# GpSimd's order in the second and fourth down projection: the last two adding transfers before the squares of X

## Chip, cores and metric

One core of a Trainium2 chip runs the whole forward pass of a small model in one launch. The metric is the device time of one launch in microseconds. The kernel before takes 1082.13 us, the median of three runs (1081.0 to 1082.24). The engines are named TensorE (PE), VectorE (DVE), ScalarE (ACT), GpSimd (POOL) and SyncE (SP), whose queue issues most loads.

## The reference

The input x has 512 tokens of 1024 features. There are two layers. The first mixes tokens by sliding-window attention, the second by gated linear attention, and each is followed by a gated feed-forward block (FFN) with 2816 hidden features:

```python
def conv_ffn(h, w_up, conv_w, conv_b, w_down):
    u = h @ w_up
    gate, up = u[..., :D_FF], u[..., D_FF:]
    ...
    return (jax.nn.silu(conv) * up) @ w_down

for i in range(DEPTH):
    h = rmsnorm(x, mix_norm[i])
    ...
    x = x + y
    x = x + conv_ffn(rmsnorm(x, ffn_norm[i]), f_w_up[i], f_conv_w[i], f_conv_b[i], f_w_down[i])
return rmsnorm(x, final_norm)
```

What matters here is `h @ w_down`, its addition to x, and the RMS norm behind it, which needs the sum of x squared over the 1024 features of each token. All is in float32.

## The kernel before

**Layout.** X lies with features on the 128 partitions, as 8 tiles of 128 x 512 (features x tokens). Every float32 matmul is made of three faster ones: operands are split into a high part (a cast, made by ScalarE) and a low part (raw minus high, made by VectorE), and high x high, high x low and low x high are summed in PSUM.

**The FFN** runs in two chunks of hidden features: 6 pairs of 128-feature tiles in the first chunk, 5 pairs in the second (`PAIRS`). For each chunk the up projection runs first and the down projection behind it. The down projection is computed with a Strassen-like scheme: the 256 x 256 block of a round is made of seven products (`PRODUCTS`: Z1, W11, W12, Z2, Z4, Z3, W22) of 128 x 256 matmuls. W11, W12 and W22 are quarters of the weight as loaded; Z1 = W21 + W22 and Z3 = W21 + W11 are sums made by transfers; Z2 = Z1 + W11 and Z4 = Z2 + W12 are sums made by VectorE (`sum_z2`, L1496; `sum_z4`, L1505).

**Rounds.** A chunk has four rounds, n to n + 3, one for each pair of X tiles. Rounds are numbered through the kernel: 0 to 3 and 4 to 7 are layer 0's two chunks, 8 to 11 and 12 to 15 layer 1's. "Second and fourth down projection" are rounds 4 to 7 and 12 to 15. TensorE's order is written out in `down_phase` (L590): within the second round of a chunk it is Z1, W22 of the round before, W11, W12, Z2, Z4, Z3, and then the next round's Z1. In a second chunk each product is 5 x 3 matmuls of 256 columns.

**The sums by transfer.** SP loads W21 into a buffer (`load_21`, L351). GpSimd waits for it (`first_half`) and issues a transfer that adds W22 or W11 to it in place (`add_quarter`, L1992). The buffers of the last round, n + 3, are loaded by SP in `load_round` (L374) when the first round's W22 is done, in the middle of the second round; those of the earlier rounds lie in GpSimd's queue before. ScalarE (`weight_hi`, L1013) and, for Z1, VectorE (`sum_z2`) wait for the added sum.

**The squares.** In a second chunk the rounds complete X tile by tile. ScalarE's `down_round` (L1073) calls `x_tile` (L972): the high part of the finished X tile in layer 0, and its square into one of two buffers SQ (L980). It writes a buffer only after GpSimd has summed the square of two tiles before. GpSimd's `sum_square` (L1974) copies square 0 to SS (L1981) and adds the others to SS (L1984). Squares 0 and 1 are of the first round's two tiles, 2 and 3 of the second's, 4 and 5 of the third's.

**VectorE's order** (`down_rounds`, L1602). Takes (`take_z4`, `take_z3` and others, L1522) add or subtract a product's PSUM bank to a half of an X tile. Between them VectorE makes the low parts of the weights (`weight_lo`, L1494), sum_z2 (L1503) and sum_z4 (L1514). In the second round m = n + 1 it goes, after take_z2: sum_z2 of m + 1, low part of Z1 of m + 1, take_z4, sum_z4 of m + 1, low part of W11 of m + 1, and then, as the next round's first step, take_z3 of m. TensorE needs the low part of Z1 before Z1 of the third round, and take_z3 before W22 of the second, which uses the same PSUM bank:

```python
def w22(n, between=None):
    pe.wait_ge(x_taken, COUNT[n, "Z3"])
    down_product(n, "W22", SETS[n % 2][0], False, between=between)
```

**GpSimd's order** is `ffn` in its block (L1987): squares 6 and 7 of the norm ahead of the FFN, then in each chunk the eight adding transfers, and in a second chunk squares among and behind them.

Of the kernel before, what the change touches and what calls it, by code (L numbers as in the profile page):

```python
# [95 lines left out]
def trunk(nc, xT, gains, w_qkv, sinks, rel_bias, w_o, w_bin, w_ga, w_gate, b_norm, w_bo, w_up, conv_w, conv_b,  # L96
          w_down0, w_down1, onehot, ident, causal, causal_pair, out, bias_rows):
    with ExitStack() as ctx:
# [202 lines left out]
        def down_cols(n):  # L301

            return PAIRS[n // 4 % 2] * P

        def quarter(n, name):

            layer, chunk, r = n // 8, n // 4 % 2, n % 4
            return (w_down0, w_down1)[chunk][layer, r, ("W11", "W12", "W21", "W22").index(name)]

        def with_sum(n, name):  # L310

            if n % 4 == 0:
                return DRAW["Z1"] if name == "Z1" else Z3RAW
            return WSUM[name, n % 4]
# [1650 lines left out]
        def _(pool):  # L1965
# [8 lines left out]
            def sum_square(st, m, par=None):  # L1974

                par = m % 2 if par is None else par
                pool.wait_ge(sq_ready, m + (KT_D * st + 1))
                if isinstance(m, int) and m == 0:
                    if st:
                        pool.wait_ge(std_ready, st)  # L1980
                    nc.gpsimd.tensor_copy(SS[:], SQ[:, 0]).then_inc(ss_ready, 1)  # L1981
                    pool.wait_ge(ss_ready, KT_D * st + 1)
                else:
                    nc.gpsimd.tensor_tensor(SS[:], SS[:], SQ[:, par], ALU.add).then_inc(ss_ready, 1)  # L1984
                    pool.wait_ge(ss_ready, m + (KT_D * st + 1))

            def ffn(layer, st):  # L1987
                for j in range(2):
                    sum_square(st, 6 + j)
                pool.wait_ge(r_ready, st + 1)  # L1990

                def add_quarter(n, name):  # L1992
                    onto, src = with_sum(n, name), "W22" if name == "Z1" else "W11"
                    pool.wait_ge(first_half[name, n % 4], 16 * (n // 4 + 1))
                    pool.dma_start(onto[:, 0:down_cols(n)], quarter(n, src), accum_op=ALU.add)\
                        .then_inc(added[name, n % 4], 16)

                for chunk in range(2):
                    n = 4 * (2 * layer + chunk)
                    for m in range(n, n + 3):  # L2000
                        add_quarter(m, "Z1")
                        add_quarter(m, "Z3")
                    if chunk:
                        sum_square(st + 1, 0)
                    add_quarter(n + 3, "Z1")
                    if chunk:
                        sum_square(st + 1, 1)
                    add_quarter(n + 3, "Z3")
                    if chunk:
                        for m in range(2, 6):  # L2010
                            sum_square(st + 1, m)
                if layer == 0:
                    for m in (6, 7):
                        sum_square(st + 1, m)
# [26 lines left out]
            for m in range(6):  # L2041
                sum_square(1, m)
            ffn(0, 1)
            pool.wait_ge(down_done, COUNT[7, "W22"])
            nc.gpsimd.memset(GAT[:].bitcast(F32), 1.0).then_inc(small_set, 2)
# [39 lines left out]
            for m in range(6):  # L2085
                sum_square(3, m)
            ffn(1, 3)

            pool.wait_ge(sq_ready, KT_D * 5 - 1)
# [88 lines left out]
```

## Time and profile before

| what | value |
|---|---|
| median of 3 runs | 1082.13 us (1081.0 to 1082.24) |
| the profiled execution's own time | 1082.68 us |
| its span, first to last instruction | 1080.9 us |
| TensorE busy | 1071.6 us, 99% |
| VectorE busy | 751.2 us, 69% |
| ScalarE busy | 494.3 us, 46% |
| GpSimd busy | 113.4 us, 10% |
| granted TensorE clock, mean | 1.000 |
| down projection, second chunk of layer 0 | from 453.31 us |
| down projection, second chunk of layer 1 | from 1020.55 us |

The durations come from one profiled execution, with times from its first instruction. Matmuls overlap each other, so that the distance between the starts of two says more than the duration of one. A row of a timeline has the start, the duration, the engine, the line of the kernel, the operation, what it writes and reads, the shapes, and in brackets the idle time before it with what ended it.

### The profile page before, as it was taken

How to read it: one execution, taken by the hardware profiler on the slowest of the kernel's cores; microseconds unless marked ns; L12 is line 12 of the kernel's file. 1: busy time of each engine (PE TensorE's matmuls, PEld its weight loads, DVE VectorE, ACT ScalarE, POOL GpSimd, SP SyncE). 2: the span in 40 equal slices, each digit the busy share in tenths (PEclk: the TensorE clock that was granted, in tenths of full speed). 3: DMA queues.
4: the chain of work that ended last, by engine and by line, in shares of the span. 5: the costliest groups of instructions: out<-in, count | busy, mean ns of one | idle time of the engine just before them, and what ended most of it. 6: DMA issues, size and time to landing. Idle time of an engine off the chain costs nothing.

```text
span 1080.9 us, 15711 instructions
## 1 busy us (share of the span) xinstructions
PE 1071.6 (99%) x5930; PEld 920.9 (85%) x5930; DVE 751.2 (69%) x1097; ACT 494.3 (46%) x769; POOL 113.4 (10%) x108
## 2 busy tenths in 40 slices
PE   9999999999999999999999999999999999999997
PEld 7888788888899888899888888888888899888897
DVE  6588667676876667789644556867676876667785
ACT  7366554444443334455661345454444433334443
POOL 1100030000100000123021221130000100000122
PEclk9999999999999999999999999999999999999999
DMA  7611032225652225652222211232226652225552
GB/s 228 153 59 60 27 111 98 97 97 184 161 145 98 96 97 170 141 154 91 79 78 98 79 40 59 66 110 98 97 97 184 161 149 97 94 97 170 139 135 91
DMA packets 43804, 121.12 MB, mean 112 GB/s; under 512 B 5250, under 2 KB 10530, under 8 KB 43748
## 3 DMA queue, kind: packets, MB, share of 16 engines
q1 hardware_dynamic: 36020, 106.55, 28.8%
q0 software_dynamic: 4608, 11.54, 6.4%
q10 hardware_dynamic: 3120, 2.28, 1.2%
q8 instruction: 37, 0.61, 0.2%
q14 instruction: 19, 0.16, 0.1%
HBM read 116.93 MB, written 2.88 MB: 111 GB/s over the span
## 4 chain that ended last, share of the span: by engine, by line
PE 96%; DVE 1%; ACT 1%; DMA 1%; issue 0%; SPq 0%; POOL 0%; DVEq 0%; POOLq 0%
PE PS L485 70%; PE PS L545 19%; PE PS L667 1%; PE PS L685 1%; PE PS L849 1%; PE PS L675 1%; DMA X<-xT 1%; PE PS L817 1%; PE PS L851 0%; PE PS L836 0%; PE PS L820 0%; PE PS L746 0%; PE PS L773 0%; PE PS L859 0%; PE PS L786 0%
## 5 line engine op out<-in xcount | busy, mean ns | idle before, releaser
L485 PE MATMUL PS<-XH,WH 128*128 128x512 f32 x992 | 391.3, 394 | 1.0 <-DVE WL L1700 0.6
L485 PE MATMUL PS<-XH,WL 128*128 128x512 f32 x992 | 386.4, 390 | 0.0
L485 PE MATMUL PS<-XL,WH 128*128 128x512 f32 x992 | 386.1, 389 | 0.0
L485 PEld LDWEIGHTS PS<-XH,WH 128*128 128x128 f32 x992 | 186.3, 188 | 41.8 <-issue 2.9
L485 PEld LDWEIGHTS PS<-XL,WH 128*128 128x128 f32 x992 | 186.3, 188 | 38.9 <-issue 1.0
L485 PEld LDWEIGHTS PS<-XH,WL 128*128 128x128 f32 x992 | 186.2, 188 | 39.0
L950 ACT CAST WH<-WRAW 128x1024 fp32r<-128x1024 f32 x134 | 139.5, 1045 | 158.1 <-DMA WRAW<-w_up 107.5
L1389 DVE TENSOR_TENSOR WL<-WRAW,WH 128x1024 fp32r<-128x1024 f32 x134 | 167.4, 1250 | 16.4 <-ACT WH L950 15.8
L1427 DVE TENSOR_TENSOR GS<-PS,R 128x512 f32<-128x512 f32 x44 | 30.4, 692 | 118.2 <-PE PS L485 118.2
L545 PE MATMUL PS<-AH,DH_Z 128*128 128x256 f32 x352 | 97.9, 278 | 0.3
L545 PE MATMUL PS<-AH,DL_Z 128*128 128x256 f32 x352 | 97.4, 277 | 0.0
L545 PE MATMUL PS<-AL,DH_Z 128*128 128x256 f32 x352 | 97.3, 277 | 0.0
L993 ACT ACTIVATE CV<-GS,CONVB,CONVW 128x512 f32<-128x512 f32 x44 | 36.0, 819 | 91.6 <-DVE GS L1427 91.6
L545 PE MATMUL PS<-AH,DH_W 128*128 128x256 f32 x264 | 73.7, 279 | 0.1
L545 PE MATMUL PS<-AL,DH_W 128*128 128x256 f32 x264 | 73.0, 277 | 0.0
L545 PE MATMUL PS<-AH,DL_W 128*128 128x256 f32 x264 | 73.0, 277 | 0.0
L1522 DVE TENSOR_TENSOR X<-X,PS 128x256 f32<-128x256 f32 x112 | 46.3, 418 | 35.2 <-PE PS L545 34.7
L545 PEld LDWEIGHTS PS<-AH,DH_Z 128*128 128x128 f32 x352 | 66.2, 188 | 2.2 <-PE PS L485 1.9
L545 PEld LDWEIGHTS PS<-AL,DH_Z 128*128 128x128 f32 x352 | 66.1, 188 | 0.0
L545 PEld LDWEIGHTS PS<-AH,DL_Z 128*128 128x128 f32 x352 | 66.1, 188 | 0.0
L1027 ACT CAST DH_W<-DRAW_W 128x768 fp32r<-128x768 f32 (+1 forms) x48 | 37.0, 780 | 53.3 <-DMA DRAW_W<-w_down 53.1
L545 PEld LDWEIGHTS PS<-AH,DH_W 128*128 128x128 f32 x264 | 49.7, 188 | 0.5 <-DVE X L1522 0.4
(236 smaller groups left out, 1513.0 us busy)
## 6 DMA issues: line engine op xcount, KB each, us to landing
WRAW<-w_up SPq DMA_DIRECT2D x88, 512.0 KB, 3.2
WRAW<-w_bin SPq DMA_DIRECT2D x24, 512.0 KB, 3.2
DRAW_W<-w_down SPq DMA_DIRECT2D x24, 384.0 KB, 3.8
DRAW_W<-w_down SPq DMA_DIRECT2D x24, 320.0 KB, 3.0
WSUM_Z<-w_down SPq DMA_DIRECT2D x12, 384.0 KB, 4.8
WSUM_Z<-w_down POOLq DMA_DIRECT2D x12, 384.0 KB, 6.1
WRAW<-w_qkv SPq DMA_DIRECT2D x8, 512.0 KB, 3.5
WSUM_Z<-w_down SPq DMA_DIRECT2D x12, 320.0 KB, 3.9
```

The costliest lines, as they stand in the source:

```text
L485: last = mm(PS[:, bank], w[:, c:c + P], x[:, kb], start=start and n == 0 and w is wh and x is hi, stop=stop and n == len(kbs) - 1 and w is wl)
L545: last = mm(PS[:, bank, 0:TH], w[:, c], act_part[:, kb, x], start=start and kb == 0 and w is DH[name] and act_part is AH, stop=kb == PAIRS ...
L667: last = mm(PS[:, B4 + k % 2, c:c + P], q, keys[:, first:first + P], start=True, stop=True)
L675: last = nc.tensor.transpose(PS[:, B6, i * P:(i + 1) * P], PB[:, k % 2, i], IDENT[:])
L685: last = mm(PS[64 * half:64 * half + 64, B7, j * P:(j + 1) * P], V[:, 1 - j if p else 0, p, g * HD:(g + 1) * HD], PT[:, k % 2, 2 * j + hal ...
L817: mm(PS[:, B4, c], EN[:, h, c], EP[:, h, c], start=True, stop=True)
L950: nc.scalar.copy(WH[s][:], WRAW[s][:]).then_inc(hi_ready, 1)
L993: A(CV[:, par], GS[:, par, 2:T + 2], ACT.Identity, bias=CONVB[:, layer, tile], scale=CONVW[:, layer, tile, 2]).then_inc(c0_ready, 1)
L1027: nc.scalar.copy(DH[name][:, c], raw[:, c]).then_inc(down_hi[name], 1)
L1389: tt(WL[s][:], WRAW[s][:], WH[s][:].bitcast(F32), ALU.subtract).then_inc(lo_ready, 1)
L1427: tt(GS[:, par, 2:T + 2], PS[:, 2 * par], R[:], ALU.mult).then_inc(unit_evac, 2)
L1522: tt(x, x, PS[:, SETS[n % 2][bank], 0:TH], op).then_inc(x_taken, 1)
```

## The change

In the second chunk of each layer GpSimd issued the adding transfers of the last round with squares 0 and 1 between them. It now issues both transfers directly behind the six before, and sums squares 0 to 5 behind them. Nothing else is changed.

```diff
@@ -2000,14 +2000,10 @@
                     for m in range(n, n + 3):
                         add_quarter(m, "Z1")
                         add_quarter(m, "Z3")
-                    if chunk:
-                        sum_square(st + 1, 0)
                     add_quarter(n + 3, "Z1")
-                    if chunk:
-                        sum_square(st + 1, 1)
                     add_quarter(n + 3, "Z3")
                     if chunk:
-                        for m in range(2, 6):
+                        for m in range(6):
                             sum_square(st + 1, m)
                 if layer == 0:
                     for m in (6, 7):
```

## Rows read from the trace of the kernel before

**Rows 1.** The page, part 1: busy time, share of the span and instructions.

```profile
PE 1071.6 (99%) x5930; PEld 920.9 (85%) x5930; DVE 751.2 (69%) x1097; ACT 494.3 (46%) x769; POOL 113.4 (10%) x108
```

**Rows 2.** Timeline of TensorE, layer 0: last matmul of Z1, first of W22.

```profile
477.22 0.28 PE L545 MATMUL PS<-AH,DL_Z 128*128 128x256 f32 x1
477.47 0.38 PE L545 MATMUL PS<-AH,DH_W 128*128 128x256 f32 x1
```

**Rows 3.** Timeline of TensorE, layer 1: around the starts of Z1 and W22.

```profile
1042.77 0.28 PE L545 MATMUL PS<-AH,DL_Z 128*128 128x256 f32 x1
1043.12 0.36 PE L545 MATMUL PS<-AH,DH_Z 128*128 128x256 f32 x1
...
1044.81 0.28 PE L545 MATMUL PS<-AH,DL_Z 128*128 128x256 f32 x1
1045.16 0.38 PE L545 MATMUL PS<-AH,DH_W 128*128 128x256 f32 x1
```

**Rows 4.** Timeline of VectorE, layer 0: sum_z2, low part of Z1, take_z3.

```profile
473.51 1.04 DVE L1503 TENSOR_TENSOR DRAW_Z<-WSUM_Z,DRAW_W 128x640 f32<-128x640 f32 x1 [0.65 <-DMA DRAW_W<-w_down]
474.47 0.81 DVE L1494 TENSOR_TENSOR DL_Z<-WSUM_Z,DH_Z 128x640 fp32r<-128x640 f32 x1
...
477.00 0.41 DVE L1522 TENSOR_TENSOR X<-X,PS 128x256 f32<-128x256 f32 x1
```

**Rows 5.** Timeline of VectorE, layer 1: the same three operations.

```profile
1040.41 1.83 DVE L1503 TENSOR_TENSOR DRAW_Z<-WSUM_Z,DRAW_W 128x640 f32<-128x640 f32 x1 [0.30 <-DMA DRAW_W<-w_down]
1042.16 0.81 DVE L1494 TENSOR_TENSOR DL_Z<-WSUM_Z,DH_Z 128x640 fp32r<-128x640 f32 x1
...
1044.70 0.41 DVE L1522 TENSOR_TENSOR X<-X,PS 128x256 f32<-128x256 f32 x1
```

**Rows 6.** Timeline of GpSimd, layer 0: square 0, transfer, square 1, transfer.

```profile
466.89 0.61 POOL L1981 COPY SS<-SQ 128x512 f32<-128x512 f32 x1 [16.42 <-ACT SQ L980]
471.67 0.86 POOL L1995 DMA_DIRECT2D WSUM_Z<-w_down  x1 [4.16 <-DMA WSUM_Z<-w_down]
472.24 1.61 POOL L1984 TENSOR_TENSOR SS<-SS,SQ 128x512 f32<-128x512 f32 x1
474.26 0.89 POOL L1995 DMA_DIRECT2D WSUM_Z<-w_down  x1 [0.41 <-POOL SS L1984]
```

**Rows 7.** Timeline of GpSimd, layer 1: transfer, square 1, transfer.

```profile
1039.34 0.88 POOL L1995 DMA_DIRECT2D WSUM_Z<-w_down  x1 [4.90 <-DMA WSUM_Z<-w_down]
1039.90 1.64 POOL L1984 TENSOR_TENSOR SS<-SS,SQ 128x512 f32<-128x512 f32 x1
1041.95 0.89 POOL L1995 DMA_DIRECT2D WSUM_Z<-w_down  x1 [0.41 <-POOL SS L1984]
```

**Rows 8.** Timeline of all engines, layer 0, third round: a square and a low part.

```profile
489.96 1.29 POOL L1984 TENSOR_TENSOR SS<-SS,SQ 128x512 f32<-128x512 f32 x1 [6.19 <-ACT SQ L980]
490.03 1.90 DVE L1494 TENSOR_TENSOR DL_Z<-DRAW_Z,DH_Z 128x640 fp32r<-128x640 f32 x1
```

**Rows 9.** SP's loads of W21 for the last round, by line: layer 0, layer 1.

```profile
L353 SPq DMA_DIRECT2D WSUM_Z<-w_down x2: 432/432/433, 467.7 to 468.2; - x2
...
DMA to landing us min/median/max: 3.3/3.9/4.4
...
L353 SPq DMA_DIRECT2D WSUM_Z<-w_down x2: 432/432/432, 1035.0 to 1035.4; - x2
...
DMA to landing us min/median/max: 3.7/3.9/4.1
```

**Rows 10.** Timeline of ScalarE: the square of tile 2, layer 0 and layer 1.

```profile
477.64 0.61 ACT L980 ACTIVATE SQ<-X 128x512 f32<-128x512 f32 x1
...
1044.70 0.63 ACT L980 ACTIVATE SQ<-X 128x512 f32<-128x512 f32 x1
```

**Rows 11.** Stretches of 20 us, L545: PE busy (starts), PEld busy (starts), clock, DMA.

```profile
479.00:499.00 20.00, 20.00 (x179) 20.00 (x178) 1.00 0.37 120
...
1046.00:1066.00 20.00, 20.00 (x173) 20.00 (x172) 1.00 0.23 67
```

## The prediction

> **What bounds the kernel.** The page comes first: TensorE works 1071.6 of the span's 1080.9 us [rows 1]. So a change can only show where TensorE waits, or where it is made to wait. The change touches the two stretches in which the second column chunk of a layer is projected down, which begin near 453 us (layer 0) and 1020 us (layer 1), and there I read TensorE's timeline. Its matmuls of 256 columns follow each other about every 0.11 us (179 in 20 us, [rows 11]). Layer 0 has one visible wait, 477.22 to 477.47, where W22 of the second round starts late [rows 2]. Layer 1 has two in the same round: Z1 of the third round starts 0.35 us behind its forerunner, and W22 of the second again 0.35 [rows 3]. That is 0.14 us lost in layer 0 and 2 x 0.24 in layer 1.
>
> VectorE's timeline says what TensorE waited for. In layer 0 it is a chain of six operations without a gap: sum_z2, the low part of Z1, take_z4, sum_z4, the low part of W11, take_z3. It starts at 473.51, when a load lands, and ends at 477.41, and W22 starts 0.06 later [rows 4]. In layer 1 the chain runs from 1040.41 to 1045.11, and W22 starts at 1045.16 [rows 5]. It is 0.8 us longer there because sum_z2 takes 1.83 us instead of 0.81.
>
> GpSimd's timeline says why. Its square 1 is on SBUF from 1039.90 to 1041.54 [rows 7], and sum_z2, which reads two SBUF tiles, ends 0.70 later at 1042.24 [rows 5]. The pattern repeats: in layer 0 square 1 ends at 473.85 [rows 6] and sum_z2 at 474.55 [rows 4]. Later a square alone takes 1.29, and the subtraction begun 0.07 behind it takes 1.90 and ends 0.68 behind the square's end [rows 8]. So a VectorE operation on two SBUF tiles waits until a GpSimd operation is done, and then needs 0.70 instead of its 0.81: they overlap by about 0.12. Issuing a transfer does not do this: 0.89 us of issue from 474.26 leaves the subtraction at 474.47 with its 0.81 [rows 4, 6].
>
> **What the change does, and its cost.** It adds and removes no instruction. In each layer, squares 0 and 1 move behind the two transfers of the last round, on GpSimd's queue alone. SP's queue keeps its order.
>
> The transfers. Z1's issue waits for a landing now and stays at 471.67 and 1039.34 [rows 6, 7]. Z3's first half was issued at 468.2 and landed 4.4 us later, at 472.6; in layer 1 1035.4 + 4.1 = 1039.5 [rows 9]. GpSimd took up Z1 0.67 us after its landing (467.7 + 3.3 = 471.0 against 471.67), so Z3 can be issued at about 473.3 instead of 474.26, and in layer 1 right behind Z1's issue, at 1040.2 instead of 1041.95. That gain of 1.0 and 1.7 us is worth nothing: these sums are read for the last round, which TensorE has not begun. Z3's 320 KB then moves while the SP loads of the next round are in flight. Bounds: nothing, or the 1.1 us by which two issues half a microsecond apart differed in landing [rows 9], on a load with slack; I take nothing.
>
> The later squares and ScalarE. Square 0 must be summed before ScalarE writes the same buffer again, at 477.64 and 1044.70 [rows 10]. By the working below it is done at 474.8 and 1041.8 to 1042.4, so this wait stays covered, by over 2 us.
>
> The later squares and VectorE, which is the cost. Square 0, a copy of 0.61 us, ran at 466.89, where VectorE had time before its next operand from TensorE, and square 1 ended just as the chain began [rows 6]. Both now fall inside the chain.
> Layer 0: sum_z2 at 473.51 is no longer held and ends at 474.32. GpSimd leaves its issue at 474.2 and starts the copy behind it: 474.32 - 0.13 + 0.61 = 474.80. The low part of Z1 ends 0.69 later, 475.49. Square 1 follows: 475.49 - 0.13 + 1.29 = 476.65. take_z4 reads PSUM and slips in. sum_z4 ends at 476.65 + 0.69 = 477.34, the low part of W11 0.73 later, 478.07, take_z3 0.33 later, 478.40. It was 477.41: TensorE loses **1.0 us**.
> Layer 1: sum_z2 goes from 1040.41 to 1041.22. The issue ends at 1041.1, so the copy and the low part of Z1 compete for the next turn. Copy first: low part 1042.4, square 1 1043.6, sum_z4 1044.3, low part of W11 1045.0, take_z3 1045.3. Low part first gives 1045.3 too. It was 1045.11: TensorE loses **0.2 us**. Its wait for Z1 goes, but the one for W22, 1.7 us on, takes all of that back.
> Bounds: no loss at all if the squares were to find gaps, and 2 x (0.61 + 1.29) = 3.8 us if both lay in the chain twice over and nothing overlapped. I take 1.2 us, the value that the rows of this very chain give.
>
> The spacing behind a wait. From 1046 to 1066 TensorE starts 173 matmuls, from 479 to 499 it starts 179 [rows 11]: 3.4% fewer, at a granted clock of 1.00 both times, so it is no matter of the clock. Over the last 23 us this is 0.8 us. It began behind the wait at 1045.16. The wait in layer 0 left none. No row tells which wait leaves it. Both waits at W22 stay in place but end elsewhere, so it can go in layer 1 (-0.8) or come in layer 0, where 23 us of down projection follow as well (+0.8). I take 0 in both layers, as each layer's own row has it.
>
> **Sum.** The profiled execution took 1082.68 us, its span 1080.9: 1082.68 + 1.0 + 0.2 = 1083.9. The median of the runs shown, 1082.13, lies 0.55 below it, and so I forecast 1083.3.
>
> The handover weighed. The rows say that the loser of a collision ends 0.68 to 0.70 us behind the winner [rows 4 to 8], so the two overlap a little. The Trainium skill (SBUF - State Buffer, "Who interferes with whom" and "A bandwidth-pool intuition that's wrong") has the loser blocked until the other's end, plus about 115 ns in its one measurement. By that figure each of the eight handovers would cost about 0.24 us more, an estimate from that page, and the sum would be near 1085.2; the rows measure this handover without that gap.
>
> **Rivals.** 0.2% is 2.2 us, about what a measurement of this kernel can tell from no change; so "faster" is below 1080.0 and "slower" above 1084.3.
> - The wide spacing goes in layer 1: 1.2 - 0.8 = 0.4 us, 1082.5. For it: two of the three waits left none. Against: the wait at the same W22 did. Chance 0.25.
> - Slower: the wide spacing comes in layer 0 as well, from W22's start at 478.5 to 501. Its price is 0.8 us, 2.0 in all, 1084.1, and it decides if the longer wait (1.1 instead of 0.14 us) restarts TensorE as the one at 1045.16 did. Against: layer 0's present wait did not. Chance 0.18, and some two fifths of it beyond the bound.
> - The handover has no overlap: the loser needs its whole 0.81 or 1.29 behind the winner, 0.12 more at each of eight places, 1.0 us in all: 1084.3. All the collisions above speak against it. Chance 0.04, and half of it slower.
> - Faster: the squares fall behind the chain. Then all that VectorE lost to square 1 comes back, 0.14 + 0.48 + 0.8 = 1.4 us: 1080.7. It needs GpSimd to be held until 477.4 and 1045.1, some 3 us longer than two issues of 0.9 take, or ScalarE's square to be late. Nothing shows that. Chance 0.08, a third of it below the bound.
> - It does nothing: VectorE's delay meets slack that I don't see, or the order of the transfers alone was changed: 1082.1. Chance 0.10; the gapless chain of [rows 4] speaks against it.
>
> **The numbers.** My forecast has 0.35. Faster: 0.08 x 1/3, 0.03. Slower: 0.18 x 0.4 + 0.02 + 0.02 from the forecast's own tail = 0.11. The same: 0.86. The range goes from 1081.3, which leaves out most of the gaining case, to 1084.5, which takes in both spacings and the slower handover.
>
> **What would show it.** In the changed profile: Z3's issue about 1 us and 1.7 us earlier; squares 0 and 1 side by side behind it, near 474.2 and 1041.1; in layer 0 the low part of Z1 and sum_z4 stretched by about 0.4 and 0.8, and W22 starting at 478.5; in layer 1 sum_z2 back at 0.81, no wait before Z1, and W22 at 1045.4 on the old scale (plus what layer 0 added). It would be wrong if VectorE's chain were not stretched in layer 0, if ScalarE waited for square 0, or if the last 20 us held 179 matmuls instead of 173.

## The result and the profile after

The changed kernel takes 1084.34 us (median of 7 runs, 1083.52 to 1086.81), the kernel before in the same comparison 1081.8 us (7 runs, 1081.0 to 1082.24). The ratio is 1.0026, with a 95% interval of 1.0016 to 1.0036: slower by about 2.5 us. The forecast was 1083.3 us and no measurable change. The profiled execution of the changed kernel took 1084.34 us, its span 1082.5 us.

The page of the changed kernel, part 1, has TensorE's busy time almost where it was [rows 1], and GpSimd, whose instructions are the same 108, at 115.7 us instead of 113.4:

```profile
PE 1072.0 (99%) x5930; PEld 921.2 (85%) x5930; DVE 753.0 (70%) x1097; ACT 494.1 (46%) x769; POOL 115.7 (11%) x108
```

The view of TensorE's waits has a new first row. Its columns are the total wait in us, how often, and the longest. Both waits are for the low part of Z1, and it had no row before:

```profile
PE PS L545 <- DVE DL_Z L1494: 2.1, 2, 1.3
```

TensorE's timeline shows where: at Z1 of the third round in each layer, and a little again at W22 of the second. These rows stand against [rows 2, 3].

```profile
475.64 0.28 PE L545 MATMUL PS<-AH,DL_Z 128*128 128x256 f32 x1
476.71 0.35 PE L545 MATMUL PS<-AH,DH_Z 128*128 128x256 f32 x1 [0.80 <-DVE DL_Z L1494]
...
478.44 0.28 PE L545 MATMUL PS<-AH,DL_Z 128*128 128x256 f32 x1
478.75 0.38 PE L545 MATMUL PS<-AH,DH_W 128*128 128x256 f32 x1
...
1044.03 0.28 PE L545 MATMUL PS<-AH,DL_Z 128*128 128x256 f32 x1
1045.57 0.36 PE L545 MATMUL PS<-AH,DH_Z 128*128 128x256 f32 x1 [1.26 <-DVE DL_Z L1494]
...
1047.30 0.28 PE L545 MATMUL PS<-AH,DL_Z 128*128 128x256 f32 x1
1047.61 0.38 PE L545 MATMUL PS<-AH,DH_W 128*128 128x256 f32 x1
```

To compare executions I count from the first matmul of the stretch (453.31 and 1020.55 before, 453.06 and 1021.83 after). W22 of the second round started 24.15 us into the stretch in layer 0 and now starts at 25.69; in layer 1 it went from 24.61 to 25.78. That is 1.54 + 1.17 = **2.7 us**. From the last matmul of layer 0's stretch (line 545) to the first of layer 1's it is 519.27 us before and after, and from the last one of layer 1's stretch to the end of the span 9.27 and 9.25. So all of the loss lies in the two stretches that the change touches.

GpSimd's timeline, both layers, against [rows 6, 7]. The row "x2" holds both issues:

```profile
471.26 0.86 POOL L1995 DMA_DIRECT2D WSUM_Z<-w_down  x1 [21.14 <-DMA WSUM_Z<-w_down]
472.55 0.87 POOL L1995 DMA_DIRECT2D WSUM_Z<-w_down  x1 [0.43 <-DMA WSUM_Z<-w_down]
473.09 0.95 POOL L1981 COPY SS<-SQ 128x512 f32<-128x512 f32 x1
474.13 1.76 POOL L1984 TENSOR_TENSOR SS<-SS,SQ 128x512 f32<-128x512 f32 x1
...
1040.51 1.78 POOL L1995 DMA_DIRECT2D WSUM_Z<-w_down  x2 [21.64 <-DMA WSUM_Z<-w_down]
1041.88 1.03 POOL L1981 COPY SS<-SQ 128x512 f32<-128x512 f32 x1
1043.00 1.75 POOL L1984 TENSOR_TENSOR SS<-SS,SQ 128x512 f32<-128x512 f32 x1
```

VectorE's timeline of the same chain, against [rows 4, 5]:

```profile
473.03 1.70 DVE L1503 TENSOR_TENSOR DRAW_Z<-WSUM_Z,DRAW_W 128x640 f32<-128x640 f32 x1 [0.19 <-DMA DRAW_W<-w_down]
474.66 1.91 DVE L1494 TENSOR_TENSOR DL_Z<-WSUM_Z,DH_Z 128x640 fp32r<-128x640 f32 x1
476.49 0.41 DVE L1522 TENSOR_TENSOR X<-X,PS 128x256 f32<-128x256 f32 x1
...
478.29 0.41 DVE L1522 TENSOR_TENSOR X<-X,PS 128x256 f32<-128x256 f32 x1
...
1041.87 1.73 DVE L1503 TENSOR_TENSOR DRAW_Z<-WSUM_Z,DRAW_W 128x640 f32<-128x640 f32 x1 [0.51 <-DMA DRAW_W<-w_down]
1043.53 1.90 DVE L1494 TENSOR_TENSOR DL_Z<-WSUM_Z,DH_Z 128x640 fp32r<-128x640 f32 x1
...
1047.15 0.41 DVE L1522 TENSOR_TENSOR X<-X,PS 128x256 f32<-128x256 f32 x1
```

Read the two side by side. In layer 0 sum_z2 starts at 473.03 and the copy (square 0) is handed out at 473.09, while GpSimd still issues Z3, until 472.55 + 0.87 = 473.42. Yet the copy is done first: it ends at 474.04, which is 0.62 after the issue, its plain duration [rows 6]. Sum_z2 ends at 474.73, 0.69 behind it. Then the turns alternate. Square 1 ends at 475.89 and the low part of Z1 at 476.57, 0.68 behind. So **both squares sit ahead of Z1's low part**, and the chain up to take_z3's end takes 478.70 - 473.03 = 5.67 us. Layer 1 has the same pattern with 5.69. Before it was 3.90 and 4.70 [rows 4, 5].

The sum closes: layer 0 has 1.77 more of chain, begun 0.23 earlier in the stretch (19.97 us into it instead of 20.20), gives 1.54; layer 1 has 0.99 more, begun 0.18 later, gives 1.17.

### The profile page after: what moved, and what is told of

Its sections match the earlier page's. It is cut to its first block, busy times and chain, and to the rows that moved or that the text cites. A ratio compares the mean times of both kernels' runs of the same rounds, so it can differ in the third digit from the quotient of the medians.

```text
span 1082.5 us, 15711 instructions
## 1 busy us (share of the span) xinstructions
PE 1072.0 (99%) x5930; PEld 921.2 (85%) x5930; DVE 753.0 (70%) x1097; ACT 494.1 (46%) x769; POOL 115.7 (11%) x108
## 4 chain that ended last, share of the span: by engine, by line
PE 95%; DVE 1%; DMA 1%; ACT 1%; issue 0%; SPq 0%; POOL 0%; DVEq 0%; POOLq 0%
PE PS L485 69%; PE PS L545 19%; PE PS L667 1%; PE PS L685 1%; DMA DRAW_W<-w_down 1%; PE PS L849 1%; PE PS L675 1%; DMA X<-xT 1%; PE PS L817 1%; PE PS L851 0%; PE PS L836 0%; PE PS L820 0%; PE PS L746 0%; DVE DL_Z L1494 0%; PE PS L773 0%; PE PS L859 0%
## 5 line engine op out<-in xcount | busy, mean ns | idle before, releaser
L545 PE MATMUL PS<-AH,DH_Z 128*128 128x256 f32 x352 | 97.9, 278 | 2.3 <-DVE DL_Z L1494 2.1
L545 PE MATMUL PS<-AL,DH_Z 128*128 128x256 f32 x352 | 97.3, 276 | 0.0
L545 PE MATMUL PS<-AH,DL_Z 128*128 128x256 f32 x352 | 97.3, 276 | 0.0
L545 PE MATMUL PS<-AH,DH_W 128*128 128x256 f32 x264 | 73.6, 279 | 0.1
L545 PE MATMUL PS<-AH,DL_W 128*128 128x256 f32 x264 | 73.0, 277 | 0.0
L545 PE MATMUL PS<-AL,DH_W 128*128 128x256 f32 x264 | 73.0, 277 | 0.0
L545 PEld LDWEIGHTS PS<-AH,DH_Z 128*128 128x128 f32 x352 | 66.2, 188 | 4.3 <-issue 2.4
L545 PEld LDWEIGHTS PS<-AL,DH_Z 128*128 128x128 f32 x352 | 66.1, 188 | 0.0
L545 PEld LDWEIGHTS PS<-AH,DL_Z 128*128 128x128 f32 x352 | 66.1, 188 | 0.0
L545 PEld LDWEIGHTS PS<-AH,DH_W 128*128 128x128 f32 x264 | 49.6, 188 | 0.5 <-DVE X L1522 0.5
```

The lines of the kernel that those rows point to most:

```text
L545: last = mm(PS[:, bank, 0:TH], w[:, c], act_part[:, kb, x], start=start and kb == 0 and w is DH[name] and act_part is AH, stop=kb == PAIRS ...
```

## The experiments

Theory: the loss comes from the squares that go ahead of sum_z2 and of Z1's low part. Rivals: the earlier transfers cost it (T in the expectations), the spacing of the matmuls alone does (S), only one layer's move or one of the two squares costs it, or whatever GpSimd has handed out by the end of an issue goes first, however small (D). All edits are to the changed kernel's order in the second chunk, and distances are again from the stretch's first matmul. Where a number of runs is given, the kernel before was run beside it: 1082.64 us (33 runs) for the first four, 1082.34 (27) for the next three, 1082.28 (26) for the last three.

**One layer at a time.** In the first kernel layer 0 has the new order and layer 1 the old one; in the second it is the other way round.

```diff
+                    if chunk and layer != 0:
+                        sum_square(st + 1, 0)
                     add_quarter(n + 3, "Z1")
+                    if chunk and layer != 0:
+                        sum_square(st + 1, 1)
                     add_quarter(n + 3, "Z3")
                     if chunk:
-                        for m in range(6):
+                        for m in range(0 if layer == 0 else 2, 6):
```

> The change in layer 0 alone; layer 1 keeps the order of before. Theory C (collisions: square 0 and square 1 are both summed inside VectorE's chain ahead of Z1 of the third round): in layer 0 sum_z2 and the low part of Z1 last about 1.7 and 1.9 us, TensorE's wait before that Z1 is 1.0 to 1.3 us, and the whole kernel is 1.5 us slower than before (1083.3). Theory T (the earlier transfers hold up SP's loads, so that sum_z2 starts late): W11 lands later than 4.5 us after its issue and sum_z2 starts over 0.5 us later than in the kernel before. Theory S (the wider spacing of matmuls alone): no wait over 0.5 us, and the loss is 0.8 us or nothing.

> The change in layer 1 alone; layer 0 keeps the order of before. Theory C: the same two stretched operations in layer 1, a wait of 1.2 to 1.4 us before Z1 of the third round, and 0.4 to 1.2 us slower than before (1082.2 to 1083.0), the lower end if the wider spacing behind W22 goes. Together with the other layer's run the losses add up to that of the whole change (2.5 us). Theory T: the losses don't add up, or sum_z2 starts late. Theory S: no wait over 0.5 us.

Layer 0 alone: 1084.2 us, ratio 1.0010 (1.0001 to 1.0019). Layer 1 alone: 1083.79, ratio 1.0009 (1.0000 to 1.0018). By these ratios each carries about 1 us; together that is 0.0019 against 0.0026 for the whole change, which the intervals allow. Each shows the pattern in its changed layer alone: sum_z2 1.73 and 1.67 us, low part of Z1 1.91 both times, a wait of TensorE before that Z1 of about 1.1 and 1.0 us, W22 at 25.47 and 25.78. Waits of that length are not a matter of spacing, so S alone falls. And layer 1, to which the forecast gave 0.2 us, costs about as much as layer 0.

**The order without the squares.** Both transfers early as in the change, but squares 0 and 1 shortened to a copy of one column into a scratch tile; square 2 begins the sum, so the first two are left out of it.

```diff
+                if short:
+                    nc.gpsimd.tensor_copy(WARM[:, 0:1], SQ[:, par, 0:1]).then_inc(ss_ready, 1)
...
-                            sum_square(st + 1, m)
+                            sum_square(st + 1, m, short=m < 2, first=m == 2)
```

> The order of the change, but squares 0 and 1 are left out of the sum: in their places GpSimd copies one column to a scratch tile, and square 2 starts the sum. Transfers, waits and order are those of the change. Theory C: the collisions go, sum_z2 and the low part of Z1 are back at 0.8 to 1.0 us, no wait over 0.3 us before Z1 or W22, and the time is 0.3 to 1.5 us below the kernel before (1080.3 to 1081.5). Theory T: still 1.5 to 2.5 us slower than before (1083.3 to 1084.3), since the transfers go out as early.

It took 1081.69 us, ratio 0.9993 (0.9984 to 1.0002). VectorE's chain, layer 0, has all its operations at their plain length:

```profile
472.83 0.83 DVE L1503 TENSOR_TENSOR DRAW_Z<-WSUM_Z,DRAW_W 128x640 f32<-128x640 f32 x1 [0.25 <-DMA DRAW_W<-w_down]
473.57 0.82 DVE L1494 TENSOR_TENSOR DL_Z<-WSUM_Z,DH_Z 128x640 fp32r<-128x640 f32 x1
```

With the transfers early and the squares out of the way the loss is gone. The rival that blames the transfers falls: their new place costs nothing that shows, and gains nothing that shows either.

**Both squares ahead of both transfers.** Everything is computed; only the order differs from the change.

```diff
+                    if chunk:
+                        sum_square(st + 1, 0)
+                        sum_square(st + 1, 1)
                     add_quarter(n + 3, "Z1")
                     add_quarter(n + 3, "Z3")
                     if chunk:
-                        for m in range(6):
+                        for m in range(2, 6):
```

> The other way round: both squares ahead of both transfers (square 0, square 1, Z1, Z3), where GpSimd otherwise waits for Z1's first half to land. Square 1 is then summed near 469.9 and 1036.2. Theory C: sum_z2 has its 0.81 us in both layers, the waits before Z1 and W22 of the second round go, and the time is 0.4 to 1.5 us below the kernel before (1080.3 to 1081.4). Theory T: as the kernel before, within 0.3 us, since Z1's transfer goes out as before and Z3's 1 us earlier. Theory S: anything between 1081 and 1083, by the spacing alone.

1082.06 us, ratio 0.9996 (0.9987 to 1.0005): the loss is gone, but the gain over the kernel before that was expected does not show. Square 1 runs at 469.39 and 1035.46, in time that VectorE has free, and sum_z2 takes 0.82 and 0.83. The same squares in another place cost nothing: it is the place that costs.

**Square 1 alone behind the transfers.** Square 0 goes ahead of them.

```diff
+                    if chunk:
+                        sum_square(st + 1, 0)
                     add_quarter(n + 3, "Z1")
                     add_quarter(n + 3, "Z3")
                     if chunk:
-                        for m in range(6):
+                        for m in range(1, 6):
```

> Only square 1 behind both transfers; square 0 stays where it was before the change. Measured by the distance from the start of the stretch's first 256-column matmul to W22 of the second round (24.16 us in layer 0 and 24.61 in layer 1 before, 25.69 and 25.78 after the change, 24.02 and 24.02 without any wait). Theory C, with the square taking its turn ahead of sum_z2 when it is dispatched while GpSimd still issues: square 1 holds sum_z2 until 0.69 us behind its end; 25.2 and 25.4, some 1.8 us slower than before in all. If instead sum_z2 keeps its turn because it has begun first: 24.6 to 24.8 in both, and sum_z2 lasts 0.82.

1084.09 us, ratio 1.0016 (1.0007 to 1.0025). W22 starts at 25.66 and 25.26. One square behind the transfers already brings more than half of the loss, and this kernel shows the order of turns most plainly. GpSimd's timeline, layer 0, the issue of Z3 and square 1:

```profile
472.88 0.87 POOL L1995 DMA_DIRECT2D WSUM_Z<-w_down  x1 [0.56 <-DMA WSUM_Z<-w_down]
473.44 1.63 POOL L1984 TENSOR_TENSOR SS<-SS,SQ 128x512 f32<-128x512 f32 x1
```

VectorE's timeline of the same moment, sum_z2:

```profile
473.39 2.37 DVE L1503 TENSOR_TENSOR DRAW_Z<-WSUM_Z,DRAW_W 128x640 f32<-128x640 f32 x1 [0.58 <-DMA DRAW_W<-w_down]
```

Sum_z2 has started 0.05 us before the square and 0.36 before the issue ends (473.75). Still the square is done first, at 475.07 = 473.75 + 1.32, and sum_z2 0.69 behind it.

**The sequence of the forecast, made by hand.** GpSimd waits for sum_z2 before it takes up the squares, so that sum_z2 keeps its turn as the prediction had it.

```diff
                     if chunk:
+                        pool.wait_ge(summed["Z2"], n + 3)
                         for m in range(6):
```

> The order of the change, but GpSimd waits for the third round's sum_z2 before square 0. This is the sequence that the prediction worked out: sum_z2 first, then the squares against the low part of Z1, sum_z4 and the low part of W11. Theory C: no wait before Z1 of the third round over 0.2 us, W22 of the second at 25.1 to 25.2 us from the stretch's start in layer 0 and in layer 1 (25.69 and 25.78 with the change), so 0.5 us per layer better than the change and 0.5 to 1.0 us per layer worse than before. If the order of the turns does not matter: 25.7 in both, as with the change.

1083.23 us, ratio 1.0008 (0.9999 to 1.0017). VectorE's timeline, layer 0:

```profile
472.81 0.82 DVE L1503 TENSOR_TENSOR DRAW_Z<-WSUM_Z,DRAW_W 128x640 f32<-128x640 f32 x1
473.54 0.82 DVE L1494 TENSOR_TENSOR DL_Z<-WSUM_Z,DH_Z 128x640 fp32r<-128x640 f32 x1
...
474.61 0.90 DVE L1514 TENSOR_TENSOR DRAW_Z<-DRAW_Z,DRAW_W 128x640 f32<-128x640 f32 x1
475.44 1.92 DVE L1494 TENSOR_TENSOR DL_W<-DRAW_W,DH_W 128x640 fp32r<-128x640 f32 x1
477.28 0.41 DVE L1522 TENSOR_TENSOR X<-X,PS 128x256 f32<-128x256 f32 x1
```

GpSimd's timeline, layer 0, squares 0 and 1:

```profile
473.69 1.15 POOL L1981 COPY SS<-SQ 128x512 f32<-128x512 f32 x1 [0.54 <-DVE DRAW_Z L1503]
474.92 1.75 POOL L1984 TENSOR_TENSOR SS<-SS,SQ 128x512 f32<-128x512 f32 x1
```

The chain takes 477.69 - 472.81 = 4.88 us; the prediction's own steps give 478.40 - 473.51 = 4.89. Its two collisions stand one turn later (at sum_z4 and the low part of W11), since GpSimd took up the copy 0.15 us behind the low part of Z1. They stretch the chain by 0.1 + 1.1 us where the prediction had 0.4 + 0.8, so the agreement is one of the sum: in both sequences take_z4 slips in beside a square once. Here, with no issue under way, the operation that had started kept its turn. W22 came at 24.63 and 24.68, earlier than expected, because W11 had landed about half a microsecond earlier (sum_z2 19.70 us into the stretch instead of 20.20): that part of the expectation missed.

**Both squares behind the chain.** GpSimd waits for take_z3 of the second round.

```diff
                     if chunk:
+                        pool.wait_ge(x_taken, COUNT[n + 1, "Z3"])
                         for m in range(6):
```

> The order of the change, but GpSimd waits for take_z3 of the second round before square 0: both squares fall behind VectorE's chain, the rival that the prediction gave 0.08. Theory C: W22 at 24.02 us in both layers (no wait), sum_z2 at 0.82. ScalarE then waits some 0.5 us for square 0 before its square 2, which has slack; time 0.3 to 1.0 us below before. If the squares only move the cost on: a wait of TensorE of over 0.3 us somewhere in the third round, and the time of before or above.

1083.07 us, ratio 1.0005 (0.9996 to 1.0014). The waits go, as expected: sum_z2 0.83 in both layers, W22 at 24.46 in both. The expected gain over the kernel before does not show. The profiled execution has the wide spacing described further down from the first W22 to the end in both stretches; how much of the missing gain that is in the other runs stays open.

**How small an operation must be.** Squares 0 and 1 become copies of 16 columns (layer 0) and 128 (layer 1) in one kernel, 256 and 1 in another, all in the place of the change.

```diff
-                    nc.gpsimd.tensor_copy(SS[:], SQ[:, 0]).then_inc(ss_ready, 1)
+                    nc.gpsimd.tensor_copy(SS[:, c], SQ[:, par, c]).then_inc(ss_ready, 1)
...
-                            sum_square(st + 1, m)
+                            sum_square(st + 1, m, cols=(16, 128)[layer] if m < 2 else T, first=m == 2)
```

> The order of the change, but in place of squares 0 and 1 GpSimd copies 16 columns of each to the sum's tile in layer 0 and 128 columns in layer 1; square 2 starts the sum afresh, so squares 0 and 1 are left out of it. The question is which of the two gets the turn when GpSimd's operation is handed out within 0.06 us of sum_z2 and behind an issue that still runs for 0.3 us. Theory D (the operation holds VectorE off from the moment it is handed out, whatever its size): sum_z2 lasts 1.0 to 1.2 us in both layers. Theory W (only a wide operation does, a narrow one waits for sum_z2): 0.82 in layer 0, and in layer 1 0.82 or about 1.2, which says on which side 128 columns lie.

> The same with 256 columns in layer 0 and one column in layer 1 (the one column now goes to the sum's tile, where the third run wrote a scratch tile). Theory D: sum_z2 lasts 1.3 to 1.5 us in layer 0 and 1.0 in layer 1. Theory W: 1.3 to 1.5 in layer 0 and 0.82 in layer 1. If one column now holds sum_z2 up, it was the scratch tile and not the width that let it pass in the third run.

One execution each, 1082.86 and 1081.49 us, read for the turns only. VectorE's sum_z2 beside 16 and 128 columns:

```profile
472.74 0.82 DVE L1503 TENSOR_TENSOR DRAW_Z<-WSUM_Z,DRAW_W 128x640 f32<-128x640 f32 x1 [0.32 <-DMA DRAW_W<-w_down]
...
1040.63 0.82 DVE L1503 TENSOR_TENSOR DRAW_Z<-WSUM_Z,DRAW_W 128x640 f32<-128x640 f32 x1
```

And beside 256 columns in the other kernel, first VectorE's timeline:

```profile
472.23 0.83 DVE L1503 TENSOR_TENSOR DRAW_Z<-WSUM_Z,DRAW_W 128x640 f32<-128x640 f32 x1
472.97 1.02 DVE L1494 TENSOR_TENSOR DL_Z<-WSUM_Z,DH_Z 128x640 fp32r<-128x640 f32 x1
```

then GpSimd's:

```profile
472.24 2.01 POOL L1982 COPY SS<-SQ 128x256 f32<-128x256 f32 x2
```

In layer 1 of that kernel the copy has one column. VectorE's timeline and GpSimd's:

```profile
1039.52 0.82 DVE L1503 TENSOR_TENSOR DRAW_Z<-WSUM_Z,DRAW_W 128x640 f32<-128x640 f32 x1 [0.23 <-DMA DRAW_W<-w_down]
...
1039.54 0.84 POOL L1982 COPY SS<-SQ 128x1 f32<-128x1 f32 x1
```

The copy ends at 1040.38, 0.04 us behind sum_z2: it waited. All the copies were handed out 0.01 to 0.06 us behind sum_z2's start, during the issue, as in the change. At 1, 16, 128 and 256 columns sum_z2 keeps its turn (at 256 it had been expected to lose it); at 512 it did not in any of the seven cases. So the rival that anything handed out during an issue goes first falls, and the width of the operation matters.

**The squares in halves.** The test of that on the whole computation: squares 0 and 1 as two operations of 256 columns each, in the place of the change.

```diff
+                parts = (slice(0, TH), slice(TH, T)) if split else (slice(0, T),)
...
-                            sum_square(st + 1, m)
+                            sum_square(st + 1, m, split=m < 2)
```

> The order of the change, with squares 0 and 1 each summed in two operations of 256 columns instead of one of 512; all is computed. If an operation of 256 columns leaves sum_z2 its turn, as the copies in the last two runs did: sum_z2 lasts 0.82 to 0.85 us, no wait before Z1 of the third round over 0.2, W22 at 24.5 to 24.9 us from the stretch's start (25.69 and 25.78 with the change), and the time is 1 to 2 us below the change. If what let sum_z2 pass there was that squares were left out and not their width: sum_z2 lasts 1.3 us or more and W22 stays at 25.5 or above.

1082.65 us, ratio 1.0004 (0.9995 to 1.0013), about 2.4 us below the change beside it. VectorE's timeline, layer 0:

```profile
473.55 0.82 DVE L1503 TENSOR_TENSOR DRAW_Z<-WSUM_Z,DRAW_W 128x640 f32<-128x640 f32 x1 [0.23 <-DMA DRAW_W<-w_down]
474.30 1.02 DVE L1494 TENSOR_TENSOR DL_Z<-WSUM_Z,DH_Z 128x640 fp32r<-128x640 f32 x1
...
476.30 1.37 DVE L1494 TENSOR_TENSOR DL_W<-DRAW_W,DH_W 128x640 fp32r<-128x640 f32 x1
```

Four operations share SBUF with the chain and still stretch it by only 0.2 + 0.6 us; W22 comes at 24.51 and 24.46 into the stretch. The order is that of the change, all squares are summed, and the loss is gone.

**The change and the squares-first order once more**, on one chip. The first kernel is the change itself, the second has the order with both squares ahead of both transfers.

> The change itself, beside the others on one chip. Theory C: W22 at 25.5 to 25.8 us in both layers; 2 to 3 us slower than before.

> Both squares ahead of both transfers, again, beside the change on one chip. Theory C: no wait in the second round; W22 at 24.02 us, or 24.46 where the spacing is wide; 2.5 to 3.5 us faster than the change, and 0 to 0.7 us faster than before.

The change: 1085.01 us (10 runs), ratio 1.0026 (1.0017 to 1.0036). Squares first: 1082.11 (11 runs), ratio 0.9999 (0.9990 to 1.0008). The slowdown repeats, and the squares-first order is 2.9 us faster than the change. It is not measurably faster than the kernel before. VectorE's sum_z2 in its layer 0 has its plain length but starts late, behind the load of W11:

```profile
473.80 0.82 DVE L1503 TENSOR_TENSOR DRAW_Z<-WSUM_Z,DRAW_W 128x640 f32<-128x640 f32 x1 [0.97 <-DMA DRAW_W<-w_down]
```

So W22 comes at 24.25 there, 0.23 later than the 24.02 of the same order in its first run: with the collision removed, the load of W11 is what ends last.

## Why the prediction was wrong

**The step that failed** is in layer 0: "sum_z2 at 473.51 is no longer held and ends at 474.32. GpSimd leaves its issue at 474.2 and starts the copy behind it." In layer 1 it is the same assumption: "sum_z2 goes from 1040.41 to 1041.22 [...] so the copy and the low part of Z1 compete for the next turn." Sum_z2 does not keep its turn. The copy, handed out during the issue, goes ahead of it, and square 1 then ahead of the low part of Z1.

**Why the two meet.** The forecast let 0.67 us pass between the landing of Z3's first half and Z3's issue, as it had read for Z1 behind a square. Behind another issue it was 0.39 (the landing events of the trace, both layers), so the issue stood 0.48 and 0.52 us ahead of sum_z2 where the forecast had 0.2. An operation queued behind the issue is handed out 0.54 to 0.56 us after the issue's start, and so just as sum_z2 starts. That is no chance: in all 28 stretches of the 14 traces the load of W11, which releases sum_z2, landed 0.75 to 0.81 us behind the load that releases Z3's issue, and in the 24 with that issue ahead of sum_z2 the two starts lie 0.48 to 0.62 us apart. Whether the copy would also win if it were handed out later during the issue, as the forecast's times have it, was not tried.

What the wrong order costs can be read from the rows. First, VectorE stands still from sum_z2's start (473.03) to the end of the issue (473.42), when by its length the copy really begins: 0.4 us. Second, in the forecast's sequence take_z4, which reads PSUM, slips in beside square 1, and that shelter of 0.33 us is lost when the square sits one turn earlier. Together 0.7 of the 5.67 - 4.89 = 0.78 us. Layer 1's forecast chain (1040.41 to 1045.3) was 4.9 us, and it measured 5.69, so it misses by the same amount. The start of the chain, set by W11's landing, moved by -0.23 and +0.18 us: noise of a load, which the forecast held at zero.

| term | forecast | measured |
|---|---|---|
| layer 0, W22 later by | 1.0 us | 1.54 us |
| layer 1, W22 later by | 0.2 us | 1.17 us |
| spacing, layer 1 | 0 | -0.78 us in the profiled execution |
| profiled execution's own time | 1083.9 us | 1084.34 us |

**What held.** The chain of VectorE bounds these stretches, and the squares' loss comes out of it. In all four collisions of the two chains after the change VectorE ends 0.68 or 0.69 us behind GpSimd, as in [rows 4 to 8]; the rival of a handover without overlap falls. With sum_z2 forced to keep its turn, the working gives 4.89 us and the chip 4.88, and that kernel costs 0.9 us by its ratio (-0.1 to 1.8) where the forecast had 1.2. Z3 is issued earlier, 19.49 instead of 20.95 us into layer 0's stretch, and that is worth nothing. ScalarE does not wait for square 0: it ends at 474.04, and ScalarE's square of tile 2 starts at 478.92.

The Trainium skill (SBUF - State Buffer, "A bandwidth-pool intuition that's wrong") has one measurement, of a transfer of GpSimd's queue that lost to a VectorE copy and was blocked until about 115 ns behind its end; the collisions of the changed kernel, between two operations, show no such gap.

**The spacing** was the second wrong step: "I take 0 in both layers, as each layer's own row has it." It is not a layer's own. After the change layer 1 has the narrow spacing (view of stretches, TensorE's starts of L545, then weight loads, granted clock, DMA):

```profile
481.00:499.00 18.00, 18.00 (x161) 18.00 (x160) 1.00 0.39 133
...
1048.00:1066.00 18.00, 18.00 (x161) 18.00 (x161) 1.00 0.24 74
```

161 in 18 us is 8.94 a us, as layer 0 had before; layer 1 had 173 in 20, 8.65 [rows 11]. And the kernel with the change in layer 1 alone, whose layer 0 has the old order, has the wide spacing in layer 0:

```profile
481.00:499.00 18.00, 18.00 (x155) 18.00 (x155) 1.00 0.38 127
```

So the one row per layer that the forecast rested on was a draw, not a property. It hid part of the loss in the profiled execution: from first matmul to last of the stretch, layer 1 lost 1.17 and gained 0.78, and the span grew by only 1.6 us where the medians grew by 2.5. The profiled executions close on this: 1082.68 + 1.54 + 1.17 - 0.78, less 0.25 for the first stretch that began earlier, is 1084.36, and 1084.34 was measured. That the median stayed below the 1084.5 at which the forecast's range ends is luck: that end was drawn for a wider spacing and a slower handover, and neither came.

**The rivals.** The faster one, squares behind the chain, does not come about by itself; made by hand it takes the waits away and shows no gain. The slower one was priced for a wide spacing in layer 0, which the profile after does not have. The time went past 0.2% by a mechanism that stood in none of them, the order of turns; the sum for it would have been 1.54 + 1.17.

## What to carry to other kernels

GpSimd was off the critical path here, and its work still took turns on SBUF with VectorE's operations on two SBUF tiles: before moving it past a wait, write out beside which of them it will land, and price each order of turns that the rows leave possible. Put such work into VectorE's own gaps (here ahead of the transfers), or cut it into narrower operations, which removed the same 2.4 us. And a feature seen once in one execution, like a spacing of matmuls, needs a second execution before it enters a sum.

## What was not expected of the hardware

**Who goes first.** A GpSimd operation of 512 columns, handed out 0.01 to 0.06 us after the start of sum_z2 and while GpSimd still issued a transfer, was done first each time (the change in both its profiled executions, the one-layer kernels, and square 1 alone in layer 0). In the same place operations of 1 to 256 columns waited for sum_z2, eight times of eight. And without an issue under way 512 columns do not win either. In the kernel in which GpSimd waits for sum_z2, VectorE's timeline and GpSimd's, layer 0, third round:

```profile
490.31 0.82 DVE L1494 TENSOR_TENSOR DL_Z<-DRAW_Z,DH_Z 128x640 fp32r<-128x640 f32 x1
...
490.34 1.94 POOL L1984 TENSOR_TENSOR SS<-SS,SQ 128x512 f32<-128x512 f32 x1 [5.96 <-ACT SQ L980]
```

The square comes 0.03 us behind the low part, which keeps its 0.82 us, and the square takes 1.94 instead of 1.29. So in these traces it took both, the 512 columns and the issue under way. The Trainium skill (SBUF - State Buffer, "Who interferes with whom") has it that issue order and not the operation's shape decides who is blocked. By the starts in the profile the measurement differs during an issue: the first to start lost, and the width decided. Whether a start in the profile is the moment at which an operation takes its turn, and why the border lies between 256 and 512 columns, was not tried and stays open.

**Two spacings of matmuls.** At a granted clock of 1.00, matmuls of 256 columns follow each other every 113 or every 118 ns (the medians of the distances of starts), for 100 matmuls or more at a stretch. The wide spacing begins where W22 of a round starts. It was drawn anew in each execution of the same order: the two profiled executions of the change have it in different parts (layer 0's first part in one, layer 1's in the other, between the W22 of the first round and that of the second). It is worth about 0.9 us in the part behind the second round's W22 (24.62 us to the stretch's last matmul with the squares shortened, 23.69 with the squares first, in layer 0).

TensorE's starts in the 14 traces show when it changes. Where TensorE did not wait at the second round's W22, the spacing stayed what it was, 13 times of 13, and 10 of these were wide from there to the end. Where it waited, 3 of 15 were wide behind it, and all seven that had been wide became narrow. So a kernel without the wait saves a few tenths of a microsecond there and often keeps a spacing that costs 0.9. That may be why the orders without a collision show no gain over the kernel before, and it may explain part of the 3 to 4 us between the fastest and the slowest run of one kernel; the unprofiled runs show no spacing, so both are argued and not shown.
